# Prompt attention scores on 64 partitions at one place of each unit, and smaller first weight pieces, in a hybrid decoder layer on one Trainium2 core

## Chip, cores and metric

The kernel runs on one core of a Trainium2 chip. The metric is the device time in microseconds (us) of one execution. Everything is float32 at the interface. Inside, TensorE (PE) takes most operands as pairs of float32r numbers, a high part "hi" and the rest "lo", so that a product of two float32 matrices becomes three products: hi·hi, hi·lo and lo·hi.

## What is computed

One decoder layer for 1024 prompt tokens and 32 sample tokens (8 sequences of 4), with shared weights. Cut to what matters here:

```python
xn = rms_norm(h, norm_g)
z = xn @ w_in                       # 1024 -> 6656 columns
u, zp, q, k, v, za, ga, gb = jnp.split(z, IN_SPLIT_POINTS, axis=-1)
ya = multiscale_pool(u_pad, pos, pool_map, pool_scale) * jax.nn.silu(zp)
q = rope(rms_norm(q ...), pos)      # 16 heads of 64
k = rope(rms_norm(k ...), pos)      # 4 key heads, 4 query heads share each
# prompt: blocks of 128 queries against the previous and the own block of 128 keys
s = einsum(q, k) * 64 ** -0.5       # per head and block: 128 x 64 times 64 x 256
pr = exp(s - m) / (sum(exp(s - m)) + exp(sink - m))
o = einsum(pr, v)
yb = o * jax.nn.silu(za)
m = sigmoid(ga) * (ya @ w_proj_pool) + sigmoid(gb) * (yb @ w_proj_attn)
h = h + m @ w_out
h = h + sigmoid(h @ w_ple_gate) * (p_l @ w_ple)
```

## The kernel before

Each engine has its own program, written out by hand in order; semaphores tie them together. The order in which a function is written is the order in which its engine works. A `wait_ge` on PE stops every later PE instruction.

**The projections.** Weights come in chunks of 256 columns, each as two pieces `raw_a` and `raw_b` of 512 KB. SP (SyncE) issues the transfers (`load_chunk`), POOL (GpSimd) splits them into `w_hi` and `w_lo` (`split`), and PE multiplies (`project` calls `products`). A tile of 128 output columns takes eight steps k; a step is nine products of 352 columns: six with `w_hi`, three with `w_lo`. They accumulate in banks 0 to 2 or 3 to 5 of PSUM (`ps`), in turn. Banks 6 and 7 are left for everything else.

**The start.** SP loads the identity, x block 0, the first weight piece, x blocks 1 and 2, the second piece, and the other x blocks. PE transposes x in units (`turn_unit`) and multiplies each at once with the first chunk (`unit_products`). ACT (ScalarE) and DVE (VectorE) make the first four k of `w_hi` and `w_lo`; POOL makes the other four (k 4 to 7) when `raw_b` has come.

**The q, k, v stage.** 45 token blocks (`token_block`, number n) go to bank `n % 6`, and ACT empties each (`take_block`). Then the first gate tile starts in banks 0 to 2 once all of them have been taken (`block_free` at `8 * PAIRS`).

**Prompt attention.** There are 32 units: 8 token blocks times 4 key heads, four query heads g to a unit. A unit's PE work lies between the steps of a projection tile, two units to a tile (`attention_half`, `after[k]` is called when step k is through). For unit u these are:
- the scores S(u, s), s = 0, 1: bank for two heads each. In `qt` a query head lies with its hi part on partitions 0 to 63 and its lo part on 64 to 127; in `kt` both halves of the partitions hold the same 64 rows of the keys, once as hi (part 0) and once as lo (part 1). Two products of 128 partitions per head give all four combinations.
- the transposes T(u, s) of the probabilities (`turn_probs`), four each, one unit later;
- the values V(u) (`values`): four products of 512 columns; the third and fourth need `pt_lo` of T(u, 1).

All of them share banks 6 and 7 in rounds: `round_of` waits on `att_read`, which counts the rounds that have been read, so that each round waits for the one before the last. In order these are S(u,0), S(u,1), T(u-1,0), T(u-1,1), V(u-1). So S(u+1,1) waits for V(u-1) to be read. ACT and DVE do the rest: DVE masks the scores (`mask_scores`), ACT takes the exponentials (`exps`), copies the transposed probabilities to `pt_hi` (`hi_probs`), DVE makes `pt_lo` (`split_probs`); V is read by ACT (`low_half`, into `kv_flat`) and then by DVE, which adds (into `ps`) and multiplies twice (into `sa`) in `gate_output`.

Of the kernel before, what the change touches and what calls it, by code (L numbers as in the profile page):

```python
# [21 lines left out]
F32 = mybir.dt.float32  # L22
F32R = mybir.dt.float32r
ALU = mybir.AluOpType
# [3 lines left out]
P = 128  # L28
D = 1024
KT = D // P  # L30
# [101 lines left out]
def round_number(kind, j, i):  # L132

    return {"rows": 6 * j, "rms": 3, "back": 9 + 3 * j}[kind] + i

# [47 lines left out]
def build(nc, xp, xs, cache_k, cache_v, state, pp, ps_, params, w_in, pool_map, w_pp, w_pa, w_out, w_ple,  # L183
          w_gate, const, masks, smask, y_p, y_s, nk_p, nv_p, npool_p, nk_s, nv_s, npool_s):
    with ExitStack() as ctx:
# [119 lines left out]
        group_done, za_done, old_put, zp_done = sem("group_done"), sem("za_done"), sem("old_put"), sem("zp_done")  # L305
        paired, block_done, block_free, s_low_done, s_added = (
# [67 lines left out]
        def _(sp):  # L374
# [10 lines left out]
            def load_half(h):  # L385
                src = w_in[512 * h:512 * h + 512, COL["k"]:COL["k"] + WC].rearrange("(k p) n -> p k n", p=P)
                sp.dma_start(raw[h][:], src).then_inc(raw_loaded[h], 16)
# [6 lines left out]
            load_half(0)  # L394
            for t in range(1, 3):
                load_x(t)
            load_half(1)
# [5 lines left out]
            sp.dma_start(state_rows[0:NB * HIST, :], state).then_inc(hist_loaded, 16)  # L403
            load_chunk(1, w_in, COL["q"])
# [148 lines left out]
        def _(pool):  # L553
# [15 lines left out]
            def chunk(n, slot, end, m=None, used=tile_done):  # L569
                if not isinstance(n, int) or n != QKV_CHUNK:  # L570
                    split(n, slot, end, 0, 0, 4, n, used)
# [19 lines left out]
            for n in range(3):  # L591
                chunk(n, n % 2, chunk_end(0) if n == 2 else 0)
# [11 lines left out]
        def _(pe):  # L604
            def project(parity, free, slot, f, src_hi, src_lo, wait_m=None, used=False, k0=0, kn=KT,
                        pieces=None, after=None, done=False):
# [6 lines left out]
                for k in range(kn):  # L613
# [5 lines left out]
                    last = products(parity, slot, f, src_hi, src_lo, k, k0, kn)  # L619
# [9 lines left out]
            def products(parity, slot, f, src_hi, src_lo, k, k0=0, kn=KT):  # L629

                wh = w_hi[:, slot, k0 + k, P * f:P * f + P]
                wl = w_lo[:, slot, k0 + k, P * f:P * f + P]
                for w, parts in ((wh, (src_hi, src_lo)), (wl, (src_hi,))):
                    for c in range(NCH):
                        for x in parts:
                            last = nc.tensor.matmul(  # L636
                                ps[:, 3 * parity + c, 0:CH], w, x[:, k, CH * c:CH * c + CH],
                                start=(k == 0 and w is wh and x is src_hi), stop=(k == kn - 1 and w is wl))
                return last
# [14 lines left out]
            def unit_products(i):  # L654
# [8 lines left out]
                if g == 0 and k % 4 == 0:  # L663
                    pe.wait_ge(piece_split[k // 4], 1)
# [84 lines left out]
            def token_block(c, p):  # L749

                n, t, slot = 9 * (c - 1) + p, PAIR_BLOCKS[p], c % 2
                if n < 6:
                    pe.wait_ge(set_free[n // 3], 1)
# [8 lines left out]
                for k in range(KT):  # L762
# [10 lines left out]
                    for a, (m, x, w) in enumerate(parts):  # L773
                        last = nc.tensor.matmul(ps[0:m, n % 6, 0:WC], x, w, start=(k == 0 and a == 0),  # L774
# [70 lines left out]
            pe.wait_ge(block_free, 8 * PAIRS)  # L845
            pe.wait_ge(s_added, PAIRS)
            for i in range(2):
                for h in range(4):
# [8 lines left out]
                    else:  # L857
                        after = {4: [lambda v=v: turn_sample_probs(v)],
# [13 lines left out]
            def scores(u, m, t, s, first=False):  # L872
# [4 lines left out]
                if s == 0:  # L877
                    pe.wait_ge(unit_loaded[kv], t * 48 + 48)
                bank = round_of("S", u, s, m, first)
# [1102 lines left out]
```

## Time and profile before

| | us |
|---|---|
| median of 3 runs | 1184.72 (1183.96 to 1185.47) |
| the profiled execution's own time | 1184.52 |
| its span, first to last instruction | 1182.7 |
| PE busy | 1173.5 (99% of the span) |
| DVE, ACT, POOL busy | 571.2, 404.4, 406.0 |

The profile is of one execution. A busy time of PE holds overlaps: matmuls are pipelined, and the end of each is modelled, so what a matmul costs is read from the distance between the starts of neighbours and not from its own duration. The span is 1.8 us shorter than the execution's time. The stages, by the stretches of the trace: the start to 41.5 us, the q, k, v stage to 178, the first gates with the sample attention to 287.7, prompt attention to 566, and the pooling branch, the projections and the output to the end.

### The profile page before, as it was taken

The numbers are of one execution on the slowest core, as the hardware profiler recorded it, in microseconds if no ns is written. First come the engines' busy times: TensorE is split into PE (matmuls) and PEld (weight loads), VectorE is DVE, ScalarE is ACT, GpSimd is POOL, SyncE is SP. The second block draws the span as 40 slices with busy tenths as digits, with TensorE's granted clock in tenths as the row PEclk, the third lists the DMA queues.
The fourth block names the chain that finished last, engine by engine and source line by source line (L and its number), as shares of the span: only waits on it lengthen the run. The fifth ranks groups of instructions, "written<-read, shape, count | busy, mean of one in ns | idle before, by whom it ended". The sixth has DMA issues, their size and how long they took to land.

```text
span 1182.7 us, 19808 instructions
## 1 busy us (share of the span) xinstructions
PE 1173.5 (99%) x7720; PEld 1156.2 (98%) x7720; DVE 571.2 (48%) x1012; ACT 404.4 (34%) x922; POOL 406.0 (34%) x187
## 2 busy tenths in 40 slices
PE   8999999999999999999999999999999999999998
PEld 7999999999999999999999999999999999999998
DVE  6567773112556555565546283852264360163322
ACT  6433333233676776766110000221130130031112
POOL 3333333333212222221345333333533443274310
PEclk9999999999999999999999999999999999999999
DMA  9425466212444434423511211063222332322211
GB/s 298 166 72 159 143 164 198 63 54 74 120 122 119 136 101 132 116 81 101 201 50 56 65 47 38 2 240 126 75 88 84 115 122 79 112 87 63 64 37 55
DMA packets 115807, 124.92 MB, mean 106 GB/s; under 512 B 14192, under 2 KB 104456, under 8 KB 115744
## 3 DMA queue, kind: packets, MB, share of 16 engines
q1 hardware_dynamic: 100935, 100.22, 27.2%
q10 hardware_dynamic: 14808, 23.82, 7.3%
q8 instruction: 44, 0.72, 0.3%
q14 instruction: 20, 0.16, 0.0%
HBM read 88.93 MB, written 37.12 MB: 107 GB/s over the span
## 4 chain that ended last, share of the span: by engine, by line
PE 98%; DMA 1%; POOL 0%; DVE 0%; ACT 0%; SPq 0%; issue 0%; DVEq 0%; ACTq 0%; POOLq 0%
PE ps L636 73%; PE ps L774 10%; PE ps L892 3%; PE ps L882 2%; PE ps L908 2%; PE ps L660 2%; PE ps L1030 1%; PE ps L736 1%; DMA raw_b<-in_w_in 1%; PE ps L999 1%; PE ps L650 0%; PE ps L840 0%; PE ps L820 0%; POOL w_lo L566 0%; ACT prob L1754 0%; POOL w_hi L564 0%
## 5 line engine op out<-in xcount | busy, mean ns | idle before, releaser
L636 PE MATMUL ps<-m_hi,w_hi 128*128 128x352 f32 x1704 | 557.1, 328 | 0.5 <-ACT sa L1593 0.5
L636 PE MATMUL ps<-m_lo,w_hi 128*128 128x352 f32 x1704 | 548.0, 322 | 0.0
L636 PE MATMUL ps<-m_hi,w_lo 128*128 128x352 f32 x1704 | 367.5, 323 | 0.0
L636 PEld LDWEIGHTS ps<-m_hi,w_hi 128*128 128x128 f32 x1704 | 320.9, 188 | 3.1 <-ACT sa L1593 0.7
L636 PEld LDWEIGHTS ps<-m_lo,w_hi 128*128 128x128 f32 x1704 | 320.5, 188 | 1.4
L564 POOL TENSOR_TENSOR w_hi<-raw_a,w_one 128x1024 fp32r<-128x1024 f32 x41 | 79.0, 1927 | 703.8 <-PE ps L636 406.3
L636 PEld LDWEIGHTS ps<-m_hi,w_lo 128*128 128x128 f32 x1704 | 291.1, 188 | 0.0
L566 POOL TENSOR_TENSOR w_lo<-raw_b,w_hi 128x1024 fp32r<-128x1024 f32 x42 | 115.2, 2743 | 3.3
L566 POOL TENSOR_TENSOR w_lo<-raw_a,w_hi 128x1024 fp32r<-128x1024 f32 x41 | 103.3, 2519 | 3.2
L774 PE MATMUL ps<-w_lo,m_hi 128*128 128x256 f32 (+1 forms) x360 | 99.4, 282 | 0.0
L564 POOL TENSOR_TENSOR w_hi<-raw_b,w_one 128x1024 fp32r<-128x1024 f32 x42 | 90.8, 2161 | 10.8 <-DMA raw_b<-in_w_in 10.8
L774 PE MATMUL ps<-w_hi,m_hi 128*128 128x256 f32 x320 | 92.3, 288 | 0.0
L774 PE MATMUL ps<-w_hi,m_lo 128*128 128x256 f32 x320 | 89.9, 281 | 0.0
L1279 DVE TENSOR_TENSOR pt_lo<-ps,pt_hi 128x512 fp32r<-128x512 f32 x64 | 44.2, 691 | 48.2 <-ACT pt_hi L1740 48.2
L1851 ACT ACTIVATE gin<-gin 128x1056 f32<-128x1056 f32 x16 | 17.4, 1088 | 144.9 <-DVE gin L1405 144.9
L1740 ACT ACTIVATE pt_hi<-ps 128x512 fp32r<-128x512 f32 x64 | 38.2, 599 | 82.2 <-PE ps L892 82.2
L774 PEld LDWEIGHTS ps<-w_lo,m_hi 128*128 128x128 f32 (+1 forms) x360 | 64.5, 179 | 0.1
L1754 ACT ACTIVATE prob<-prob,st 128x257 f32<-128x257 f32 x128 | 63.4, 501 | 0.0
L1269 DVE CUSTOM_DVE_ANT_0 prob<-ps,msk,sinks_n 128x256 f32<-128x256 f32 x128 | 56.7, 481 | 9.5 <-issue 9.1
L774 PEld LDWEIGHTS ps<-w_hi,m_lo 128*128 128x128 f32 x320 | 60.5, 189 | 0.0
L774 PEld LDWEIGHTS ps<-w_hi,m_hi 128*128 128x128 f32 x320 | 60.2, 188 | 0.1
L1767 ACT ACTIVATE prob<-prob,st 128x256 f32<-128x256 f32 x128 | 54.3, 497 | 0.1
(238 smaller groups left out, 1392.6 us busy)
## 6 DMA issues: line engine op xcount, KB each, us to landing
raw_a<-in_w_in SPq DMA_DIRECT2D x26, 512.0 KB, 4.0
raw_b<-in_w_in SPq DMA_DIRECT2D x26, 512.0 KB, 4.3
qk_d<-qkst ACTq DMA_DIRECT2D x20, 512.0 KB, 5.6
gate_d<-gst ACTq DMA_DIRECT2D x16, 528.0 KB, 3.5
gin<-gate_d SPq DMA_DIRECT2D x16, 528.0 KB, 3.7
qt<-qk_d SPq DMA_DIRECT2D x32, 256.0 KB, 3.6
yb_d<-sa SPq DMA_DIRECT2D x1, 4224.0 KB, 13.8
sa<-yb_d SPq DMA_DIRECT2D x1, 4224.0 KB, 15.7
```

Source lines behind the costliest of these rows:

```text
L564: hi_count.did(nc.gpsimd.tensor_tensor(hi, raw[piece][:], one, ALU.mult))
L566: nc.gpsimd.tensor_tensor(lo, raw[piece][:], hi.bitcast(F32), ALU.subtract)\
L636: last = nc.tensor.matmul(ps[:, 3 * parity + c, 0:CH], w, x[:, k, CH * c:CH * c + CH], start=(k == 0 and w is wh and x is src_hi), stop=(k ...
L660: return nc.tensor.matmul(ps[:, 3 * h + g, 0:n], wt[:, 0, k, P * h:P * h + P], x[:, k, c0:c0 + n], start=start, stop=(k == KT - 1 and x is ...
L774: last = nc.tensor.matmul(ps[0:m, n % 6, 0:WC], x, w, start=(k == 0 and a == 0), stop=(k == KT - 1 and a == len(parts) - 1))
L882: last = nc.tensor.matmul(ps[:, bank, 256 * (g % 2):256 * (g % 2) + 256], qt[:, slot, g, :], kt[:, kv, part, :, :].rearrange("p s n -> p ( ...
L892: last = nc.tensor.transpose(ps[:, bank, P * g:P * g + P], prob[:, m % 2, g, P * s:P * s + P], ident)
L1269: last = v.tensor_tensor_reduce(prob[:, slot, g, 0:2 * P], ps[:, bank, 256 * (g % 2):256 * (g % 2) + 256], msk[:, mask, :], -1.0, sinks_n[ ...
L1279: v.tensor_tensor(pt_lo[s][:], ps[:, bank, :], pt_hi[s][:].bitcast(F32), ALU.subtract)\
L1740: a.activation(pt_hi[s][:], ps[:, bank, :], ACT.Copy).then_inc(pt_hi_done, 1)
L1754: last = a.activation(prob[:, slot, g, 0:2 * P + 1], prob[:, slot, g, 0:2 * P + 1], ACT.Exp, bias=st[:, slot, 0, g:g + 1], scale=-1.0, acc ...
L1767: last = a.activation(prob[:, slot, g, 0:2 * P], prob[:, slot, g, 0:2 * P], ACT.Copy, scale=st[:, slot, 5, g:g + 1])
```

## The change

1. **Scores.** `qt` now holds, on each half of the partitions, two of the four heads: partitions 0 to 63 heads 0 and 1, partitions 64 to 127 heads 2 and 3, each as hi and lo next to each other. A head takes three products of 64 partitions (hi·hi, lo·hi, hi·lo; lo·lo is dropped). The twelve products of a unit alternate between the halves, and with them between banks 6 and 7, and all stand at one place. The transfer of `qt` becomes four of 64 partitions.
2. **Places.** `fine` calls after each third product, not only after a step. Unit by unit: scores after step k0, T(u-1,0) nine products later, T(u-1,1) six products after that, V(u-1) six products after that; then 15 products to the next scores.
3. **ACT's order.** The exponentials of the first two heads come ahead of `hi_probs`, the other two behind it.
4. **First pieces.** The first chunk comes in four quarters of 256 KB. ACT and DVE split the first (k 0 and 1), POOL the other three.
5. **Bank of a token block.** `(n + 3) % 6` instead of `n % 6`. ACT frees banks 3 to 5 before 0 to 2 at the start; the last three blocks now lie in banks 3 to 5, and the first gate tile waits for 37 taken blocks instead of 40.

```diff
+def block_bank(n):
+    return (n + 3) % 6
...
+            def load_quarter(i):
+                src = w_in[256 * i:256 * i + 256, COL["k"]:COL["k"] + WC].rearrange("(k p) n -> p k n", p=P)
+                h, second = divmod(i, 2)
+                sp.dma_start(raw[h][:, 2 * second:2 * second + 2, :], src)\
+                    .then_inc(raw_loaded[h] if second else early_raw[h], 16)
...
             load_x(0)
-            load_half(0)
+            load_quarter(0)
             for t in range(1, 3):
                 load_x(t)
-            load_half(1)
+            for i in range(1, 4):
+                load_quarter(i)
...
-                sp.dma_start(qt[:, m % 2, :, :].bitcast(F32),
-                             qk_d[G * kv:G * kv + G, :, tok].rearrange("g p n -> p g n")).then_inc(unit_loaded[kv], 16)
+                for half in range(2):
+                    for s in range(2):
+                        sp.dma_start(qt[HD * half:HD * half + HD, m % 2, 2 * s:2 * s + 2, :].bitcast(F32),
+                                     qk_d[G * kv + 2 * half:G * kv + 2 * half + 2, HD * s:HD * s + HD, tok]
+                                     .rearrange("g e n -> e g n")).then_inc(unit_loaded[kv], 16)
...
+            def split_quarter(i):
+                h, second = divmod(i, 2)
+                pool.wait_ge(raw_loaded[h] if second else early_raw[h], 16)
+                src = raw[h][:, 2 * second:2 * second + 2, :]
+                hi, lo = w_hi[:, 0, 2 * i:2 * i + 2, :], w_lo[:, 0, 2 * i:2 * i + 2, :]
...
-            pe.wait_ge(block_free, 8 * PAIRS)
+            pe.wait_ge(block_free, blocks_taken(PAIRS, 5))
...
-                for g in (2 * s, 2 * s + 1):
-                    for part in range(2):
-                        last = nc.tensor.matmul(ps[:, bank, 256 * (g % 2):256 * (g % 2) + 256], qt[:, slot, g, :],
-                                                kt[:, kv, part, :, :].rearrange("p s n -> p (s n)"),
-                                                start=(part == 0), stop=(part == 1))
-                last.then_inc(att_done, 1)
+                banks = [round_of("S", u, s, m, first) for s in range(2)]
+                for g in range(2):
+                    for a, (q_part, k_part) in enumerate(((0, 0), (1, 0), (0, 1))):
+                        for s in range(2):
+                            half = slice(HD * s, HD * s + HD)
+                            last = nc.tensor.matmul(ps[:, banks[s], 256 * g:256 * g + 256],
+                                                    qt[half, slot, 2 * q_part + g, :],
+                                                    kt[half, kv, k_part, :, :].rearrange("p s n -> p (s n)"),
+                                                    start=(a == 0), stop=(a == 2))
+                            if g == 1 and a == 2:
+                                last.then_inc(att_done, 1)
...
-                after = {k0: [], k0 + 1: [], k0 + 2: [], k0 + 3: []}
-                after[k0].append(lambda: scores(u, m, t, 0, first and m == 0))
-                after[k0 + 1].append(lambda: scores(u, m, t, 1, first and m == 0))
+                fine = {3 * k0 + 2: [lambda: scores(u, m, t, first and m == 0)]}
                 if not first or m >= 1:
-                    after[k0 + 1].append(lambda: turn_probs(u - 1, (m - 1) % 8, 0))
-                    after[k0 + 2].append(lambda: turn_probs(u - 1, (m - 1) % 8, 1))
-                    after[k0 + 3].append(lambda: values(u - 1, (m - 1) % 8, t if m % 4 else t - 1))
+                    fine[3 * k0 + 5] = [lambda: turn_probs(u - 1, (m - 1) % 8, 0)]
+                    fine[3 * k0 + 7] = [lambda: turn_probs(u - 1, (m - 1) % 8, 1)]
+                    fine[3 * k0 + 9] = [lambda: values(u - 1, (m - 1) % 8, t if m % 4 else t - 1)]
...
                     u = i * 8 + m
+                    exps(u, m, 0)
                     if not first or m >= 1:
                         u_slot[0] = (m - 1) % 8
                         hi_probs(u - 1)
-                    exps(u, m)
+                    exps(u, m, 1)
```

PE, second unit of the attention stage, in the kernel before (L882 are the scores, L636 the projection's products, L892 the transposes, L908 the values; shapes are those of the result):

```order
L882 MATMUL ps<-kt,qt 128x256 [waits att_read,unit_loaded1]
L882 MATMUL ps<-kt,qt 128x256 x3
L636 MATMUL ps<-m_hi,w_hi 128x352
L636 MATMUL ps<-m_lo,w_hi 128x352
L636 MATMUL ps<-m_hi,w_hi 128x352
L636 MATMUL ps<-m_lo,w_hi 128x352
L636 MATMUL ps<-m_hi,w_hi 128x352
L636 MATMUL ps<-m_lo,w_hi 128x352
L636 MATMUL ps<-m_hi,w_lo 128x352 x3
L882 MATMUL ps<-kt,qt 128x256 [waits att_read]
L882 MATMUL ps<-kt,qt 128x256 x3
L892 MATMUL ps<-con_s,prob 128x128 [waits att_read,prob_done]
```

The same place with the change (L915 are the scores, L663 the products, L927 the transposes):

```order
L915 MATMUL ps<-kt,qt 128x256 [waits att_read,unit_loaded1]
L915 MATMUL ps<-kt,qt 128x256 x11
L663 MATMUL ps<-m_hi,w_hi 128x352
L663 MATMUL ps<-m_lo,w_hi 128x352
L663 MATMUL ps<-m_hi,w_hi 128x352
L663 MATMUL ps<-m_lo,w_hi 128x352
L663 MATMUL ps<-m_hi,w_hi 128x352
L663 MATMUL ps<-m_lo,w_hi 128x352
L663 MATMUL ps<-m_hi,w_lo 128x352 x3
L927 MATMUL ps<-con_s,prob 128x128 [waits att_read,prob_done]
```

Eight products at two places have become twelve at one, and both waits of the scores now stand ahead of the first of them.

PE, from the second set of transposes to the values in the same unit, before:

```order
L892 MATMUL ps<-con_s,prob 128x128 [waits att_read]
L892 MATMUL ps<-con_s,prob 128x128 x3
L636 MATMUL ps<-m_hi,w_hi 128x352
L636 MATMUL ps<-m_lo,w_hi 128x352
L636 MATMUL ps<-m_hi,w_hi 128x352
L636 MATMUL ps<-m_lo,w_hi 128x352
L636 MATMUL ps<-m_hi,w_hi 128x352
L636 MATMUL ps<-m_lo,w_hi 128x352
L636 MATMUL ps<-m_hi,w_lo 128x352 x3
L908 MATMUL ps<-pt_hi,vt 128x512 [waits zero_done,v_loaded0,att_read]
L908 MATMUL ps<-pt_lo,vt 128x512
L908 MATMUL ps<-pt_hi,vt 128x512 [waits att_read]
```

And with the change (L943 are the values):

```order
L927 MATMUL ps<-con_s,prob 128x128 [waits att_read]
L927 MATMUL ps<-con_s,prob 128x128 x3
L663 MATMUL ps<-m_hi,w_lo 128x352 x3
L663 MATMUL ps<-m_hi,w_hi 128x352
L663 MATMUL ps<-m_lo,w_hi 128x352
L663 MATMUL ps<-m_hi,w_hi 128x352
L943 MATMUL ps<-pt_hi,vt 128x512 [waits zero_done,v_loaded0,att_read]
L943 MATMUL ps<-pt_lo,vt 128x512
L943 MATMUL ps<-pt_hi,vt 128x512 [waits att_read]
```

Between these transposes and the first product of the values stand six projection products instead of nine.

SP's first transfers, before:

```order
L392 DMA con_s<-in_const 128x128
L390 DMA xr<-in_x_prompt 128x1024
L387 DMA raw_a<-in_w_in 128x4x256
L390 DMA xr<-in_x_prompt 128x1024 x2
L387 DMA raw_b<-in_w_in 128x4x256
L390 DMA xr<-in_x_prompt 128x1024 x5
```

And with the change:

```order
L400 DMA con_s<-in_const 128x128
L398 DMA xr<-in_x_prompt 128x1024
L394 DMA raw_a<-in_w_in 128x2x256
L398 DMA xr<-in_x_prompt 128x1024 x2
L394 DMA raw_a<-in_w_in 128x2x256
L394 DMA raw_b<-in_w_in 128x2x256 x2
L398 DMA xr<-in_x_prompt 128x1024 x5
```

256 KB instead of 512 KB of weights now stand ahead of x blocks 1 and 2.

## Rows read from the trace of the kernel before

**Rows 1.** The page: span, busy time of each engine, and the chain by engine.

```profile
span 1182.7 us, 19808 instructions
...
PE 1173.5 (99%) x7720; PEld 1156.2 (98%) x7720; DVE 571.2 (48%) x1012; ACT 404.4 (34%) x922; POOL 406.0 (34%) x187
...
PE 98%; DMA 1%; POOL 0%; DVE 0%; ACT 0%; SPq 0%; issue 0%; DVEq 0%; ACTq 0%; POOLq 0%
```

**Rows 2.** The attention stretch: us, busy time of PE, PEld, DVE, ACT, POOL, clock, DMA.

```profile
287.70:566.00 278.30, 278.07 (x1808) 269.21 (x1807) 156.55 (x510) 193.77 (x530) 71.58 (x34) 1.00 0.40 111
```

**Rows 3.** Timeline, one unit: start, length, engine, line, operation, count, idle before.

```profile
408.58 0.63 PE L882 MATMUL ps<-kt,qt 128*128 128x256 f32 x4
409.11 0.66 PE L892 MATMUL ps<-con_s,prob 128*128 128x128 f32 x4
...
411.05 0.60 PE L892 MATMUL ps<-con_s,prob 128*128 128x128 f32 x4
...
411.65 0.32 PE L636 MATMUL ps<-m_lo,w_hi 128*128 128x352 f32 x1
...
412.32 0.69 DVE L1279 TENSOR_TENSOR pt_lo<-ps,pt_hi 128x512 fp32r<-128x512 f32 x1 [1.20 <-ACT pt_hi L1740]
...
412.95 0.40 PE L908 MATMUL ps<-pt_hi,vt 128*128 128x512 f32 x1
...
413.41 0.39 PE L908 MATMUL ps<-pt_hi,vt 128*128 128x512 f32 x1
...
413.64 0.40 PE L908 MATMUL ps<-pt_lo,vt 128*128 128x512 f32 x1
...
413.88 0.32 PE L636 MATMUL ps<-m_hi,w_hi 128*128 128x352 f32 x1
...
414.27 0.60 ACT L1761 ACTIVATE kv_flat<-ps 64x512 f32<-64x512 f32 x1
...
415.31 0.64 PE L882 MATMUL ps<-kt,qt 128*128 128x256 f32 x4
...
415.79 0.32 PE L636 MATMUL ps<-m_hi,w_hi 128*128 128x352 f32 x1
...
415.81 0.85 DVE L1293 TENSOR_TENSOR sa<-ps,sa 64x256 f32 x2
```

**Rows 4.** Timeline around products on 64 partitions (L822) and on 32 (L837).

```profile
190.45 0.28 PE L820 MATMUL ps<-kts,q_pair 128*128 128x128 f32 x1
190.66 0.29 PEld L822 LDWEIGHTS ps<-q_sum 64*128 64x128 f32 x2
...
190.99 0.19 PEld L636 LDWEIGHTS ps<-m_hi,w_hi 128*128 128x128 f32 x1
...
191.26 0.32 PE L636 MATMUL ps<-m_lo,w_hi 128*128 128x352 f32 x1
...
204.19 0.32 PE L636 MATMUL ps<-m_hi,w_lo 128*128 128x352 f32 x1
204.44 0.29 PEld L837 LDWEIGHTS ps<-spt,v_group 32*128 32x128 f32 x2 [0.22 <-issue]
...
204.66 0.27 PE L837 MATMUL ps<-spt,v_group 32*128 32x128 f32 x1
204.86 0.19 PEld L840 LDWEIGHTS ps<-spt,vc 128*128 128x128 f32 x1
```

**Rows 5.** Timeline of the start: idle times of PE, and POOL's split.

```profile
8.75 0.88 PE L650 MATMUL ps<-con_s,xr 128*128 128x128 f32 x6 [1.47 <-DMA xr<-in_x_prompt]
10.08 0.88 PE L650 MATMUL ps<-con_s,xr 128*128 128x128 f32 x6 [0.23 <-DMA xr<-in_x_prompt]
...
16.07 0.19 PEld L660 LDWEIGHTS ps<-m_hi,w_hi 128*128 128x128 f32 x1 [0.28 <-POOL w_lo L566]
```

**Rows 6.** Timeline where the first gate tile begins.

```profile
177.97 0.43 PE L636 MATMUL ps<-m_hi,w_hi 128*128 128x352 f32 x1 [0.46 <-ACT sa L1593]
```

**Rows 7.** Timeline of SP: what issuing two transfers of 64 partitions takes.

```profile
401.29 1.31 SPq L454 DMA_DIRECT2D kt<-qk_d  x2
```

More of the change, by code:

```diff
@@ L305, in build @@
         group_done, za_done, old_put, zp_done = sem("group_done"), sem("za_done"), sem("old_put"), sem("zp_done")
+        early_raw, early_split = ([sem(f"early_{x}{i}") for i in range(2)] for x in ("raw", "split"))
         paired, block_done, block_free, s_low_done, s_added = (
@@ L569, in chunk @@
             def chunk(n, slot, end, m=None, used=tile_done):
-                if not isinstance(n, int) or n != QKV_CHUNK:
-                    split(n, slot, end, 0, 0, 4, n, used)
+                split(n, slot, end, 0, 0, 4, n, used)
                 split(n, slot, end, 1, 4, 4, n, used)
@@ L589, in chunks @@
                 hi_count.leave(count // 2 - 1, steps)
-            for n in range(3):
-                chunk(n, n % 2, chunk_end(0) if n == 2 else 0)
+            def split_quarter(i):
[3 more added lines that the diff above has]
+                hi, lo = w_hi[:, 0, 2 * i:2 * i + 2, :], w_lo[:, 0, 2 * i:2 * i + 2, :]
+                hi_count.did(nc.gpsimd.tensor_tensor(hi, src, w_one[:, 0:1].unsqueeze(2).to_broadcast([P, 2, WC]),
+                                                     ALU.mult))
+                hi_count.settle()
+                nc.gpsimd.tensor_tensor(lo, src, hi.bitcast(F32), ALU.subtract)\
+                    .then_inc(piece_split[h] if second else early_split[h], 1)
+            for i in range(1, 4):
+                split_quarter(i)
+            chunk(1, 1, 0)
+            chunk(2, 0, chunk_end(0))
             for n in range(3, GATE_CHUNK):
@@ L618, in project @@
                         pe.wait_ge(m_ready, wait_m + (k + 1))
-                    last = products(parity, slot, f, src_hi, src_lo, k, k0, kn)
+                    last = products(parity, slot, f, src_hi, src_lo, k, k0, kn, fine)
                     if used and k < kn - 1:
@@ L638, in products @@
                                 start=(k == 0 and w is wh and x is src_hi), stop=(k == kn - 1 and w is wl))
+                            count += 1
+                            if fine and count % 3 == 0:
+                                for call in fine.get(3 * k + count // 3 - 1, ()):
+                                    call()
                 return last
@@ L773, in token_block @@
                     for a, (m, x, w) in enumerate(parts):
-                        last = nc.tensor.matmul(ps[0:m, n % 6, 0:WC], x, w, start=(k == 0 and a == 0),
+                        last = nc.tensor.matmul(ps[0:m, block_bank(n), 0:WC], x, w, start=(k == 0 and a == 0),
                                                 stop=(k == KT - 1 and a == len(parts) - 1))
@@ L870, in round_of, with scores @@
                 return 6 + (att_bank(kind, m, first) + s) % 2
-            def scores(u, m, t, s, first=False):
+            def scores(u, m, t, first=False):
                 slot, kv = m % 2, m % 4
@@ L1154, in add_sample_rows @@
                 dve.wait_ge(s_low_done, c)
[L1155 removed]
+                bank = block_bank(9 * (c - 1) + 4)
                 parts = ps[0:NS, bank, 0:WC].rearrange("p (s n) -> p s n", s=2)
```

55 lines of the change are left out of this document (27 added, 28 removed).

## The prediction

> **What bounds the kernel now.** I read the page first. The reader should see in [rows 1] that PE is busy 99% of the span and makes up 98% of the chain that ended last, while no other engine reaches half. So whatever shortens PE's own work, or one of its few idle times, shortens the kernel, and whatever makes PE wait lengthens it one for one. The stretch of attention [rows 2] then shows the same for the stage that the change edits most: 278.07 us busy of 278.30, at full clock. PE waits for nobody there now. The timeline of a unit [rows 3] gives prices as distances between starts. A unit's eight score products cost 0.48 us at one place (415.31 to 415.79) and 0.53 at the other (408.58 to 409.11), so 1.01 in all; one of them is 0.12 (0.48/4). A projection product is 0.162 ((412.95 - 411.65)/8). The start [rows 5] and the first gate tile [rows 6] hold the idle times that the change could remove.
>
> **The start.** PE waits 1.47 and 0.23 us for x blocks 1 and 2. Between their arrivals 512 KB more have come in 1.33 us (8.75 to 10.08), so 256 KB less in front of them bring both forward by 0.67. The other wait, 0.28 for POOL's split of k 4 to 7, goes if POOL keeps up with quarters: it can begin with the quarter right behind x block 2, while now it waits for the whole second piece, and the work for two k is half of that for four. Gain together 0.9; bounds 0 (the transfers come in another order) and 1.2.
>
> **Banks and the first gate tile.** PE's 0.46 us wait for ACT [rows 6] is for the last taken block. With the last three blocks in banks 3 to 5 and 37 instead of 40 required, it goes: 0.5. At the other end ACT now frees banks 3 to 5 first, behind eight history transposes of PE that cover the copy; without that cover it would cost one copy, a few tenths. I take 0.
>
> **Transfers of `qt`.** Four of 64 partitions instead of one of 128. Two such take SP 1.31 us to issue [rows 7], so three more are about 2 us per unit. SP issues a unit's loads two units ahead (about 17 us, a unit being 278/32 = 8.7), and it has only seven transfers a unit to issue. The weights' loads queue behind them by 2 us, and POOL splits one chunk in two tiles. No cost.
>
> **The scores themselves.** Two terms.
> First the switch. [Rows 4] hold the only products of fewer than 128 partitions. Going in: L820 starts at 190.45, the next weight load could start then, but the load for the 64-partition product starts at 190.66, 0.21 later; for L837 the previous product starts at 204.19, its stream ends at 204.35, and the load begins at 204.44, so that the first product starts about 0.20 late. Coming out: two of these loads take 0.29 where one takes 0.19, so the second starts at 190.76 and its product at 190.86, yet the next load waits until 190.99 (0.13); behind L837's second product (204.66) the load that would normally start with it starts at 204.86 (0.20). In and out cost 0.34 and 0.40; I take 0.37 per unit, where the 128-partition scores pay nothing (starts run through at 0.12 and 0.16).
> Second the twelve products. Nothing in this trace has two products on different halves next to each other, so the bounds are: six pairs side by side, 6 x 0.12 = 0.72; or all twelve one after the other, 12 x 0.12 = 1.44. In between, weight loads in a row: two of them on 64 partitions stand 0.10 apart [rows 4], so twelve are 1.20. Nearest rows are of products that all used one half; they say nothing against two halves at once, and the alternation uses two banks and two sets of rows. I take the pairs, at odds of about three to two.
> A unit then costs 0.72 + 0.37 = 1.09 against 1.01: +0.08, times 32 = +2.6 us. One after the other it is 1.20 + 0.37 = 1.57 (+0.56, +18 us) to 1.44 + 0.37 = 1.81 (+0.80, +26 us).
> The Trainium skill ("TensorEngine Tiling (Array Packing)", Key Properties) says that different tiles can run weight loads and matmuls in parallel, and that changing the tiling mode drains the engine. By the first half of the rule the sum is that of the pairs; by [rows 4] alone, with loads in a row, it would be 15 us more. This trace agrees with the second half (0.34 and 0.40) and shows nothing of the first.
>
> **The waits that move.** The chain behind T(u-1,1) has a fixed length. From the start of its transposes (411.05) to the end of DVE's `pt_lo` (412.32 + 0.69 = 413.01) it is 1.96 us, with ACT and DVE free. PE now reaches the third product of V at 413.41, 2.36 after, so there is 0.4 of slack. With six products in between instead of nine, PE is there at (411.65 - 0.16 - 411.05) + 6 x 0.162 + 0.46 = 1.87, and its weight load should start 0.11 before that, at 1.76. The load waits behind the semaphore: a stall of 0.2, 31 times, +6 us. ACT and DVE don't gain or lose here: the exponentials of the first two heads end ahead of this copy, the others come after it.
> The chain behind V: from the start of its last product (413.64) to the end of DVE's multiplication (415.81 + 0.85 = 416.66) it is 3.02, in which ACT started 0.23 after the product's end (413.64 + 0.40 to 414.27). With two exponentials behind `hi_probs` instead of four ACT is free, so about 2.82. S(u+1,1) waits for this; now it stands a whole step behind S(u+1,0), so that it has slack. With both banks wanted at once, PE is there after 0.24 + 15 x 0.162 = 2.67, and after the 0.09 that emptying the array takes (204.35 to 204.44) the load could start at 2.76. A stall of 0.1, 31 times, +3 us. Queued behind either stall is all of PE's work; no other engine waits for it in a way that the chain would show. Lower bound of both 0, if ACT and DVE are a little quicker than in this unit; upper bound twice as much.
>
> **The sum.** Against the profiled execution, 1184.5 (span 1182.7 and 1.8 around it; the median of the runs is 1184.7): 1184.5 - 0.9 - 0.5 + 2.6 + 6 + 3 = 1194.7. I say 1195.
>
> **The rivals.**
> - *No overlap of the halves* (or the weight loads in a row): 1194.7 + 15 to + 23 = 1210 to 1218. For it: loads 0.10 apart on one half are all that the trace has. Against it: 64 partitions leave half of the array free, and the twelve products alternate so that neighbours share neither rows nor bank.
> - *Pairs and no stalls*: 1184.5 - 1.4 + 2.6 = 1185.7, no change. For it: the two stalls are differences of 0.1 and 0.2 us between chains of 2 to 3. Against it: 1.96 for the `pt_lo` chain is made of operations that waited for nothing else.
> - *Faster: the switch costs nothing next to pairs.* If a pair's first load can start while the 128-partition products drain, the scores cost 0.72 for 1.01, so -0.29 x 32 = -9.3; with the gains of the start and without stalls 1174, with both stalls 1183. It decides from the point where the switch in and out costs under 0.3 us and the stalls stay under half of what I gave them. Against it stand the four transitions of [rows 4], each 0.13 to 0.21.
> - *The change does not bring twelve products down to pairs because nothing sets the array up for halves.* Then the twelve run one by one without a switch: 12 x 0.12 - 1.01 = 0.43, +13.8, with the start's gains and both stalls 1206. L822's 0.21 speaks against it.
>
> **How the numbers follow.** Pairs with stalls (1189 to 1200) 0.45; no overlap, with or without stalls (1201 to 1218) 0.30; pairs without stalls (1182 to 1188) 0.12; the fast case 0.08; the rest, such as no switch and no overlap, 0.05. The predicted time is that of the first. The range goes from 1184 to 1217: it takes in the no-overlap case but for its edge, and most of the case without stalls. The likeliest case has 1189 to 1200 of its own. A measurement of this kernel tells 0.2% (2.4 us) from no change, so: faster 0.10, same 0.10, slower 0.80.
>
> **What would show it.** Scores: in the timeline the twelve L915 products either start in pairs a few ns apart, the group of twelve about 0.6 us long from first to last start, or 0.10 to 0.12 apart, 1.1 to 1.3 us long. The switch: the load behind them starts 0.1 after the last stream. Stalls: PE idle in front of L943 with DVE `pt_lo` as releaser, and in front of L915 with DVE `sa`, which [rows 1] had nowhere. Start: x block 2's transposes at about 9.4 instead of 10.08, and no wait for POOL's `w_lo`. First gate tile: no idle time. It would be wrong if the switch were free, if the halves did not overlap, or if the two stalls did not appear.

## The result and the profile after

The changed kernel takes 1197.07 us (median of 4 runs, 1196.62 to 1197.63) against 1184.39 for the kernel before (1183.96 to 1185.47). The ratio is 1.0105, 95% interval 1.0092 to 1.0117. So it is 12.7 us slower. The forecast was 1195 in a range of 1184 to 1217.

The page of the changed kernel (span 1195.0 us): busy times, and the chain by engine.

```profile
PE 1185.8 (99%) x7848; PEld 1148.3 (96%) x7848; DVE 565.5 (47%) x1012; ACT 405.6 (34%) x922; POOL 408.8 (34%) x191
...
PE 94%; DVE 3%; ACT 1%; issue 1%; DVEq 0%; DMA 0%; ACTq 0%
```

PE is "busy" 99% in both kernels [rows 1] and yet this one waits. What gives it away is the chain, where PE fell from 98% to 94% while DVE rose from 0% to 3% and ACT from 0% to 1%, and PEld, the weight loads, which fell from 98% of the span to 96%. The ends of matmuls are modelled, and one that started before a wait covers it. A wait of 0.2 us is seen on the loads, not on the products. The waits of PEld, with total, times and longest:

```profile
PEld ps L943 <- DVE pt_lo L1312: 12.7, 31, 0.4
PEld ps L915 <- DVE sa L1326: 8.3, 24, 0.4
...
PEld ps L915 <- issue: 2.6, 8, 0.7
```

31 times in front of the third product of the values, and 24 + 8 in front of the scores. An idle time of 0.41 here is not 0.41 lost, since a load is also idle while the product ahead streams. What is lost is read from distances. One unit of the changed kernel, cut where it says `...` (L943 values, L915 scores, L927 transposes, L663 projection products):

```profile
408.56 0.39 PE L943 MATMUL ps<-pt_lo,vt 128*128 128x512 f32 x1
...
410.52 0.85 DVE L1326 TENSOR_TENSOR sa<-ps,sa 64x256 f32 x2
...
410.72 0.65 PE L663 MATMUL ps<-m_hi,w_lo 128*128 128x352 f32 x3
...
411.42 0.78 PEld L915 LDWEIGHTS ps<-kt,qt 64*128 64x128 f32 x12 [0.35 <-DVE sa L1326]
411.42 0.98 PE L915 MATMUL ps<-kt,qt 64*128 64x256 f32 x12
412.33 0.19 PEld L663 LDWEIGHTS ps<-m_hi,w_hi 128*128 128x128 f32 x1
...
412.60 0.32 PE L663 MATMUL ps<-m_lo,w_hi 128*128 128x352 f32 x1
...
415.28 0.60 PE L927 MATMUL ps<-con_s,prob 128*128 128x128 f32 x4
...
416.55 0.69 DVE L1312 TENSOR_TENSOR pt_lo<-ps,pt_hi 128x512 fp32r<-128x512 f32 x1 [0.70 <-ACT pt_hi L1773]
...
416.93 0.40 PE L943 MATMUL ps<-pt_lo,vt 128*128 128x512 f32 x1
417.29 0.19 PEld L943 LDWEIGHTS ps<-pt_hi,vt 128*128 128x128 f32 x1 [0.41 <-DVE pt_lo L1312]
...
417.63 0.39 PE L943 MATMUL ps<-pt_lo,vt 128*128 128x512 f32 x1
```

- From the transposes' start to the end of `pt_lo`: 415.28 to 416.55 + 0.69 = 417.24, 1.96 us, exactly as before [rows 3]. The load that waits for it starts at 417.29. The second and the fourth product of the values now start 0.70 apart (416.93 to 417.63), where it was 0.46 before (2 x 0.23 [rows 3]): 0.24 lost in each unit.
- From the last product of the values to the end of DVE's multiplication: 408.56 to 411.37, 2.81. The scores' load starts at 411.42. The last projection product ahead of it starts at 411.05 (410.72 + 0.65 - 0.32) and streams until 411.21.
- From that 411.21 to the next projection product's stream (412.60 - 0.16 = 412.44) the scores cost 1.23, against 1.01 at two places before: 0.22 more, of which about 0.12 is waiting (where nothing holds it, the load starts 0.09 after the stream's end, as in e3 below; that would be 411.30, and it starts at 411.42).

The unit is 9.07 us long (408.56 to 417.63), for 8.7 before. Now the start, and where the first gate tile begins (L805 is the last product of the q, k, v stage, L769 the last transpose of q's last pair, L841 the first transposes of the keys, later in the same gate tile):

```profile
9.07 0.82 PE L681 MATMUL ps<-con_s,xr 128*128 128x128 f32 x6
...
10.18 0.41 PE L691 MATMUL ps<-m_hi,w_hi 128*128 128x384 f32 x1 [0.28 <-ACT m_hi L1579]
...
175.76 0.28 PE L805 MATMUL ps<-w_hi,m_lo 128*128 128x256 f32 x1
...
175.91 0.41 PE L663 MATMUL ps<-m_hi,w_hi 128*128 128x352 f32 x1
...
179.70 1.29 DVE L1182 TENSOR_TENSOR qkst<-ps,qkst 128x512 fp32r<-128x512 f32 x2 [2.03 <-ACT qkst L1642]
...
180.45 0.33 PE L769 MATMUL ps<-con_s,sa 128*128 128x128 f32 x1 [0.52 <-DVE qkst L1182]
...
184.97 0.60 PE L841 MATMUL ps<-con_s,kc 128*128 128x128 f32 x4
```

The same place in the kernel before (L774, L738 and L810 are those three products):

```profile
177.13 0.28 PE L774 MATMUL ps<-w_hi,m_lo 128*128 128x256 f32 x1
...
181.07 1.29 DVE L1149 TENSOR_TENSOR qkst<-ps,qkst 128x512 fp32r<-128x512 f32 x2 [2.03 <-ACT qkst L1609]
...
181.84 0.31 PE L738 MATMUL ps<-con_s,sa 128*128 128x128 f32 x1
...
186.34 0.60 PE L810 MATMUL ps<-con_s,kc 128*128 128x128 f32 x4
```

x block 2's transposes start at 9.07 instead of 10.08 [rows 5]. The first gate tile starts without a wait: 0.15 behind the last product of the stage (175.76 to 175.91), for 0.84 before (177.13 to 177.97 [rows 6]), so 0.69 is gained. But 4.5 us later PE waits 0.52 for DVE before the last transpose of q's last pair (L769), a wait that the trace of before doesn't list. DVE's operation for it starts 3.94 behind the last product of the stage in both kernels (175.76 to 179.70, 177.13 to 181.07). Only PE comes sooner, and the gain is given back in full: from the last product of the stage to the keys' transposes it is 9.21 in both (175.76 to 184.97, 177.13 to 186.34).

### The profile page after: what moved, and what is told of

Its sections match the earlier page's. It is cut to its first block, busy times and chain, and to the rows that moved or that the text cites. A ratio compares the mean times of both kernels' runs of the same rounds, so it can differ in the third digit from the quotient of the medians.

```text
span 1195.0 us, 20288 instructions
## 1 busy us (share of the span) xinstructions
PE 1185.8 (99%) x7848; PEld 1148.3 (96%) x7848; DVE 565.5 (47%) x1012; ACT 405.6 (34%) x922; POOL 408.8 (34%) x191
## 4 chain that ended last, share of the span: by engine, by line
PE 94%; DVE 3%; ACT 1%; issue 1%; DVEq 0%; DMA 0%; ACTq 0%
PE ps L663 68%; PE ps L805 10%; PE ps L943 3%; PE ps L915 3%; PE ps L927 2%; PE ps L691 2%; DVE ps L1321 1%; PE ps L1063 1%; ACT kv_flat L1796 1%; DVE sa L1326 1%; PE ps L681 1%; PE ps L767 1%; PE ps L1032 1%; PE ps L871 0%; PE ps L714 0%
## 5 line engine op out<-in xcount | busy, mean ns | idle before, releaser
L663 PE MATMUL ps<-m_hi,w_hi 128*128 128x352 f32 x1704 | 558.1, 328 | 0.0
L663 PE MATMUL ps<-m_lo,w_hi 128*128 128x352 f32 x1704 | 548.2, 322 | 0.0
L663 PE MATMUL ps<-m_hi,w_lo 128*128 128x352 f32 x1704 | 370.2, 325 | 0.0
L663 PEld LDWEIGHTS ps<-m_hi,w_hi 128*128 128x128 f32 x1704 | 320.9, 188 | 6.4
L663 PEld LDWEIGHTS ps<-m_lo,w_hi 128*128 128x128 f32 x1704 | 320.5, 188 | 1.4
L663 PEld LDWEIGHTS ps<-m_hi,w_lo 128*128 128x128 f32 x1704 | 290.1, 188 | 0.0
L805 PE MATMUL ps<-w_lo,m_hi 128*128 128x256 f32 (+1 forms) x360 | 99.4, 282 | 0.0
L805 PE MATMUL ps<-w_hi,m_hi 128*128 128x256 f32 x320 | 92.2, 288 | 0.0
L805 PE MATMUL ps<-w_hi,m_lo 128*128 128x256 f32 x320 | 89.9, 281 | 0.0
L805 PEld LDWEIGHTS ps<-w_lo,m_hi 128*128 128x128 f32 (+1 forms) x360 | 64.5, 179 | 0.1
L805 PEld LDWEIGHTS ps<-w_hi,m_lo 128*128 128x128 f32 x320 | 60.5, 189 | 0.0
L805 PEld LDWEIGHTS ps<-w_hi,m_hi 128*128 128x128 f32 x320 | 60.2, 188 | 0.1
```

Of the source, the lines that this page charges most:

```text
L663: last = nc.tensor.matmul(ps[:, 3 * parity + c, 0:CH], w, x[:, k, CH * c:CH * c + CH], start=(k == 0 and w is wh and x is src_hi), stop=(k ...
L805: last = nc.tensor.matmul(ps[0:m, block_bank(n), 0:WC], x, w, start=(k == 0 and a == 0), stop=(k == KT - 1 and a == len(parts) - 1))
```

## The experiments

Each is an edit of the changed kernel, or of an experiment that is named. The diffs are cut to what matters. Times are medians; the kernel before took 1184.2, 1184.4 and 1184.1 us in the three groups of runs.

**e1. The attention of before.** Only quarters and banks are left of the change; the products of the scores and the one transfer of `qt` are also those of before.

```diff
-                fine = {3 * k0 + 2: [lambda: scores(u, m, t, first and m == 0)]}
+                after[k0].append(lambda: scores(u, m, t, 0, first and m == 0))
+                after[k0 + 1].append(lambda: scores(u, m, t, 1, first and m == 0))
...
-                    exps(u, m, 0)
                     if not first or m >= 1:
                         u_slot[0] = (m - 1) % 8
                         hi_probs(u - 1)
-                    exps(u, m, 1)
+                    exps(u, m)
```

> The changed kernel with the attention of before (scores on 128 partitions at two places, one transfer for qt, the exponentials behind hi_probs); the quarters and the bank shift stay. My theory, from the changed kernel's trace: the start is worth about 1.1 us (first product at 10.18 instead of 11.23), and the bank shift 0, because the 0.5 us that PE no longer waits for ACT at the first gate tile comes back as 0.52 us before L769, which waits for DVE. So about 1183.3. As I predicted before the result: 1.4 us for both, 1183.0. The rival that makes the first pieces worthless, since the gain is lost further on: 1184.4.

1183.6 us, ratio 0.9990 (0.9981 to 0.9999); the span is 1181.6 for 1182.7. PE waits 0.5 us before that late transpose here too. So the start and the banks together are worth 0.6 us by the medians, 1.1 by the spans and 1.2 by the ratio: the kernel before has some runs at 1185.5 to 1186.4 which the median leaves out. The attention costs the changed kernel 13.5 us (1197.07 - 1183.6).

**e2. Second transposes three products earlier.**

```diff
-                    fine[3 * k0 + 7] = [lambda: turn_probs(u - 1, (m - 1) % 8, 1)]
+                    fine[3 * k0 + 6] = [lambda: turn_probs(u - 1, (m - 1) % 8, 1)]
```

> The changed kernel, with the second set of transposes three products earlier (nine products between it and the values instead of six, three instead of six behind the first set). Theory of the stall: PE's 0.24 us wait in front of the third product of the values goes in each of 31 units, 7.4 us, so about 1189.7. Rival, the 64-partition products themselves carry the loss: 1197, no change. Rival, T1 now waits for the masks of the second score bank: also 1197 or worse.

1189.73 us, ratio 1.0044 (1.0028 to 1.0059): 7.3 us less than the changed kernel. The wait before L943 is gone from the list, that before the scores is the same (first row), and the load of the third product starts with the second product, at 414.38:

```profile
PEld ps L915 <- DVE sa L1326: 8.4, 24, 0.4
```

```profile
414.38 0.19 PEld L943 LDWEIGHTS ps<-pt_hi,vt 128*128 128x128 f32 x1
```

One number in the source carries more than half of the loss.

**e3. Everything else of a unit earlier.**

```diff
-                    fine[3 * k0 + 5] = [lambda: turn_probs(u - 1, (m - 1) % 8, 0)]
-                    fine[3 * k0 + 7] = [lambda: turn_probs(u - 1, (m - 1) % 8, 1)]
-                    fine[3 * k0 + 9] = [lambda: values(u - 1, (m - 1) % 8, t if m % 4 else t - 1)]
+                    fine[3 * k0 + 4] = [lambda: turn_probs(u - 1, (m - 1) % 8, 0)]
+                    fine[3 * k0 + 5] = [lambda: turn_probs(u - 1, (m - 1) % 8, 1)]
+                    fine[3 * k0 + 8] = [lambda: values(u - 1, (m - 1) % 8, t if m % 4 else t - 1)]
```

> The changed kernel with the first transposes six products behind the scores, the second three behind them, the values nine behind these, and so 18 products to the next scores. Theory of the stalls: both waits go (0.24 in front of the values, 0.12 in front of the scores), 31 x 0.36 = 11 us, so 1186. If the first set then waits for ACT or DVE, only part of it: 1190. Rival, the 64-partition scores carry the loss: 1197.

1190.57 us, ratio 1.0052 (1.0036 to 1.0067), the middle one of the three cases. Both old waits are gone, but the first transposes wait:

```profile
409.65 0.32 PE L663 MATMUL ps<-m_lo,w_hi 128*128 128x352 f32 x1
...
409.90 0.42 PEld L927 LDWEIGHTS ps<-con_s,prob 128*128 128x128 f32 x4 [0.22 <-DVE st L1302]
...
416.10 0.64 PE L663 MATMUL ps<-m_hi,w_lo 128*128 128x352 f32 x3
...
416.67 0.77 PEld L915 LDWEIGHTS ps<-kt,qt 64*128 64x128 f32 x12 [0.22 <-issue]
...
417.85 0.32 PE L663 MATMUL ps<-m_lo,w_hi 128*128 128x352 f32 x1
```

The projection's stream ends at 409.65 + 0.16 = 409.81, the transposes' at best begins at 409.90 + 0.11 = 410.01: 0.20 lost in this unit. The scores, now without a wait, cost 417.85 - 0.16 - (416.10 + 0.64 - 0.32 + 0.16) = 1.11.

**e4. The eight products on 128 partitions, at the one place.** The old layout and the one transfer of `qt` come with them.

```diff
-                    for a, (q_part, k_part) in enumerate(((0, 0), (1, 0), (0, 1))):
-                        for s in range(2):
-                            half = slice(HD * s, HD * s + HD)
-                            last = nc.tensor.matmul(ps[:, banks[s], 256 * g:256 * g + 256],
-                                                    qt[half, slot, 2 * q_part + g, :],
-                                                    kt[half, kv, k_part, :, :].rearrange("p s n -> p (s n)"),
-                                                    start=(a == 0), stop=(a == 2))
+                for s in range(2):
+                    for g in range(2):
+                        for part in range(2):
+                            last = nc.tensor.matmul(ps[:, banks[s], 256 * g:256 * g + 256], qt[:, slot, 2 * s + g, :],
+                                                    kt[:, kv, part, :, :].rearrange("p s n -> p (s n)"),
+                                                    start=(part == 0), stop=(part == 1))
...
```

> The changed kernel with the scores of before, eight products of 128 partitions and the old layout of qt, but still at one place and with the changed places of everything else. My theory: the group costs 8 x 0.12 = 0.96 instead of 1.11, so 0.15 a unit less, minus a scores' stall that grows by 0.09 since PE arrives without having to empty: 32 x 0.06 = 2 us less, 1195. Rival, the switch and the 64-partition products carry the loss: 11 us less, 1186.

1197.96 us, ratio 1.0112 (1.0097 to 1.0128). Not 2 us less but 0.9 more. The waits are the changed kernel's, to 0.1 us:

```profile
PEld ps L937 <- DVE pt_lo L1306: 12.8, 31, 0.4
PEld ps L911 <- DVE sa L1320: 8.3, 24, 0.4
```

```profile
409.09 0.39 PE L937 MATMUL ps<-pt_lo,vt 128*128 128x512 f32 x1
...
411.96 1.01 PEld L911 LDWEIGHTS ps<-kt,qt 128*128 128x128 f32 x8 [0.35 <-DVE sa L1320]
...
413.01 0.32 PE L660 MATMUL ps<-m_hi,w_hi 128*128 128x352 f32 x1
```

The chain behind the values sets the instant of the scores' first load in both kernels: 2.87 after the last product of the values here (409.09 to 411.96), 2.86 in the changed kernel (408.56 to 411.42). Whatever going in costs there lies inside that wait. From the load to the next projection product it is 1.05 here (411.96 to 413.01) and 1.02 there (411.42 to 412.44): what the pairs gain, coming out takes back. The halves and the switch cost nothing *with the places of the changed kernel*; there the places make the whole loss.

**e5. Six products of the lower half, then six of the upper.** The same twelve.

```diff
-                for g in range(2):
-                    for a, (q_part, k_part) in enumerate(((0, 0), (1, 0), (0, 1))):
-                        for s in range(2):
...
+                for s in range(2):
...
+                    for g in range(2):
+                        for a, (q_part, k_part) in enumerate(((0, 0), (1, 0), (0, 1))):
...
```

> The changed kernel with the same twelve products of 64 partitions, but first the six of the lower half, then the six of the upper half, so that no neighbours but one pair use different halves. Theory of the pairs: the group grows from 0.72 to 1.44 less one product, +0.6 a unit, +19 to +22 us: 1216 to 1219. Rival, the halves overlap whatever the order is, since the queue looks ahead: 1197. The stall of the values stays; that of the scores too.

1208.09 us, ratio 1.0201 (1.0185 to 1.0216): 11 us more, between the two expectations.

```profile
415.67 1.11 PEld L915 LDWEIGHTS ps<-kt,qt 64*128 64x128 f32 x12 [0.35 <-DVE sa L1325]
...
416.92 0.19 PEld L663 LDWEIGHTS ps<-m_hi,w_hi 128*128 128x128 f32 x1
```

From the first load to the one behind the group it is 1.25, where it was 0.91 with the halves in turn (411.42 to 412.33): 0.34 x 32 = 10.9. Twelve loads within 1.11, less one load's 0.18, are 0.085 apart, closer than the 0.12 of one product behind the other on one half. So part of the upper half's products ran beside the lower half's, though they stand behind them in the program.

**e6. ACT's old order.**

```diff
-                    exps(u, m, 0)
                     if not first or m >= 1:
                         u_slot[0] = (m - 1) % 8
                         hi_probs(u - 1)
+                    exps(u, m, 0)
                     exps(u, m, 1)
```

> The changed kernel, with all four exponentials behind hi_probs on ACT, as before. Theory: hi_probs of the first set starts earlier, which nobody needs; the copy for V (low_half) waits for two more exponentials, about 0.5 to 1 us longer behind the transposes, so it starts some 0.2 us later than PE's values allow, and the stall in front of the scores grows from 0.12 to about 0.3: +5 us, 1202. Rival, ACT's order is without effect: 1197.

1210.54 us, ratio 1.0222 (1.0207 to 1.0238): 13.5 us more, where 5 were expected.

```profile
413.89 0.39 PE L943 MATMUL ps<-pt_lo,vt 128*128 128x512 f32 x1
...
414.16 0.50 ACT L1788 ACTIVATE prob<-prob,st 128x257 f32<-128x257 f32 x1
...
414.77 0.59 ACT L1796 ACTIVATE kv_flat<-ps 64x512 f32<-64x512 f32 x1
...
417.21 0.78 PEld L915 LDWEIGHTS ps<-kt,qt 64*128 64x128 f32 x12 [0.80 <-DVE sa L1326]
```

ACT is at its exponentials until 414.7 and takes up the values' result 0.88 us after the last product's start (413.89 to 414.77) instead of the 0.42 that are possible (408.56 to 408.98 in the changed kernel). The wait before the scores grows from 0.35 to 0.80, and 0.45 x 31 = 14. With ACT's old order the change of places would have cost as much again.

**e7. e3's places with e4's products.**

> Scores of before on 128 partitions, all eight at one place, and everything else three to six products earlier as in e3. Theory: without stalls, against the kernel before only the start's gain is left, and the group of eight costs the same as its two halves: 1183.3. Against e3 it shows what the halves cost with the switch: 0.15 x 32 = 5 us. Rival, scores at one place hold PE up by themselves: above 1187.

1180.64 us, ratio 0.9968 (0.9957 to 0.998): faster than the kernel before by 3.7 us, 9.9 under e3 and 3.0 under e1, which keeps the places of before. That is 2.7 less than expected.

```profile
413.44 1.11 PE L911 MATMUL ps<-kt,qt 128*128 128x256 f32 x8
...
414.39 0.32 PE L660 MATMUL ps<-m_hi,w_hi 128*128 128x352 f32 x1
...
415.19 0.32 PE L660 MATMUL ps<-m_lo,w_hi 128*128 128x352 f32 x1
...
415.36 0.60 PE L921 MATMUL ps<-con_s,prob 128*128 128x128 f32 x4
```

Everything runs through: the scores cost 0.95 (413.44 to 414.39), the transposes follow the projection product by 0.17. Against e3 that is 1.11 - 0.95 = 0.16 from the halves with their switch, 5.1 us in 32 units. The wait of the first transposes in e3 is 0.15 on average over the units (0.20 in the one shown), 4.7 us in 31. Together that is 9.8 for the measured 9.9.

The 3.0 us under e1 are a wait that the kernel before has in its attention, and e1 too. The list of waits doesn't show it:

```profile
408.56 0.48 DVE L1269 CUSTOM_DVE_ANT_0 prob<-ps,msk,sinks_n 128x256 f32<-128x256 f32 x1
...
409.10 0.42 PEld L892 LDWEIGHTS ps<-con_s,prob 128*128 128x128 f32 x4
```

T(u-1,0) stands directly behind S(u,1) and needs the bank of S(u,0), which DVE reads twice (`mask_scores`). The second reading ends at 408.56 + 0.48 = 409.04, and the load of the transposes starts 0.06 later. In 24 of the 31 units of the trace, from the eighth on, it follows by 0.06 or 0.07 as here. From the last projection product to the next, S(u,1) and T(u-1,0) together take 1.02 on average, where S(u,0) alone takes 0.47 and T(u-1,1) alone 0.44: 0.11 lost, 31 times 3.4 us. With the transposes six products behind the scores this is gone. So the sentence of the prediction that PE waits for nobody in this stage was not right: a busy PE had covered the wait.

**e8. e1 with the late transpose one step later.**

```diff
-                            after[1] = [lambda: turn("back", 9, 2)]
+                            after[2] = [lambda: turn("back", 9, 2)]
```

> As e1 (attention of before, quarters and bank shift), and the last of the three transposes of q's last pair one step (nine products) later in the first gate tile. Theory: the bank shift's 0.5 us was given back at this wait, so it now stays: 0.5 us under e1, 1182.8. Rival: it is given back once more further on, same as e1.

1182.82 us, ratio 0.9987 (0.9978 to 0.9996), 0.8 under e1; the wait is gone and the spans differ by 1.0 (1181.6 and 1180.6). The intervals of e1 and e8 overlap; the trace is clearer:

```profile
175.86 0.28 PE L802 MATMUL ps<-w_hi,m_lo 128*128 128x256 f32 x1
...
184.32 0.60 PE L838 MATMUL ps<-con_s,kc 128*128 128x128 f32 x4
```

From the last product of the q, k, v stage to the keys' transposes it is 8.46, where it was 9.21 in the kernel before and in the changed kernel: the 0.75 is kept.

**e9. e7 with e8's edit.**

> e7 (scores of before at one place, everything else of a unit earlier, quarters and bank shift) with the later transpose of e8. Theory: both gains add, 0.8 us under e7's 1180.6, so 1179.8 to 1180.2. Rival: PE's wait in front of that transpose is made up for later, 1180.6.

1180.39 us, ratio 0.9964 (0.9952 to 0.9976). The fastest of all, though not to be told from e7, and 0.2 us above what was expected.

**e10. e7 with the banks in turn.** Eight products on 128 partitions, in the order bank 6, bank 7, bank 6 and so on.

```diff
-                for s in range(2):
-                    for g in range(2):
-                        for part in range(2):
+                for g in range(2):
+                    for part in range(2):
+                        for s in range(2):
...
```

> e7, but the eight products of 128 partitions alternate between the two banks, so that the first bank is complete at the seventh product instead of the fourth. Theory of the late bank: DVE's first mask starts 0.35 us later, and the first transposes, which now find their bank read just in time, wait about 0.25 us in each of 31 units: +7 to +8 us over e7, 1188. Rival: e3's 10 us over e7 are all from the products on halves and the switch, and the order of the banks has no effect: 1180.6.

1187.98 us, ratio 1.0029 (1.0019 to 1.004): 7.3 us over e7, from nothing but the order of the same eight products.

```profile
418.66 0.32 PE L660 MATMUL ps<-m_lo,w_hi 128*128 128x352 f32 x1
...
418.99 0.42 PEld L922 LDWEIGHTS ps<-con_s,prob 128*128 128x128 f32 x4 [0.30 <-DVE st L1297]
```

The transposes' stream begins at 419.10 and could at 418.82: 0.28 lost in this unit, which 31 times would be 8.7. DVE's reading of the first bank is again what the transposes wait for.

**e11. e3's twelve products in two groups.**

```diff
-                fine = {3 * k0 + 2: [lambda: scores(u, m, t, first and m == 0)]}
+                fine = {3 * k0 + 1: [lambda: scores(u, m, t, 0, first and m == 0)],
+                        3 * k0 + 2: [lambda: scores(u, m, t, 1, first and m == 0)]}
```

> e3 with the twelve products on halves in two groups of six, three projection products between them (the first group stands three products earlier). Theory of the switch: one more switch in and out per unit, 0.37 to 0.40 us, plus about 0.1 of wait in front of the first group, since it stands nearer to the values: 32 x 0.37 + 31 x 0.1 = 15 us over e3, 1203 to 1206. Rival, the switch is only seen behind very short products and costs nothing next to pairs of 256 columns: 1191 to 1194.

1206.7 us, ratio 1.0186 (1.0171 to 1.0202), 16.1 over e3.

```profile
415.15 0.32 PE L663 MATMUL ps<-m_lo,w_hi 128*128 128x352 f32 x1
...
415.54 0.42 PEld L919 LDWEIGHTS ps<-kt,qt 64*128 64x128 f32 x6 [0.36 <-DVE sa L1331]
...
416.09 0.75 PE L663 MATMUL ps<-m_hi,w_lo 128*128 128x352 f32 x3
...
417.32 0.19 PEld L663 LDWEIGHTS ps<-m_hi,w_hi 128*128 128x128 f32 x1
```

The first group costs 416.09 + 0.11 - (415.15 + 0.16) = 0.89 and the second 417.32 + 0.11 - (416.09 + 0.75 - 0.33 + 0.16) = 0.76, together 1.65 where one group of twelve costs 1.11. 0.14 of the 0.54 is the wait for the values (0.36 idle for the 0.22 of a load that waits for nothing, as in e3), 0.40 is one more switch in and out.

## Why the prediction was right

It was 1195 (1194.7 worked out) for 1197.07 measured, with the likeliest case as the mechanism: the pairs form, and both waits appear where they were expected. Step by step:

- **Pairs.** Right. Twelve products take 0.98 from first start to last end, which less a product's modelled 0.28 and the first load's 0.11 is five steps of 0.12. Two in a pair start within 0.02 of each other. e5 shows what the order brings: 11 us of the 23 (32 x 0.72) that pairs save against twelve products one after the other; in e5 a part of the pairs still forms. The rule of the Trainium skill ("TensorEngine Tiling (Array Packing)", Key Properties) on tiles that load and multiply in parallel agrees with the loads here: twelve within 0.78 us, 0.055 apart.
- **The switch.** 0.37 was taken from four transitions of very short products; 0.40 was measured for one more (e11), and 0.16 for halves with switch against whole rows (e3 with e7), where 1.09 - 0.96 = 0.13 stood in the prediction's terms. Against the 1.01 of the two places, the term was +0.08, and the group without a wait measured 1.11, so +0.10.
- **The wait before the values.** 0.2 predicted, 0.24 measured by the distances; 6 us predicted, 7.3 by e2. The chain of 1.96 us was the same to 0.01.
- **The wait before the scores.** 0.1 predicted, about 0.12 measured; the chain of 2.82 came out as 2.81. What e4 adds: the emptying of the array lies inside this wait. In the prediction both stood in the sum, correctly, since the load can start only when both are over, but taking the halves away gains nothing then. So with the places as changed the waits are the cause of the slowdown, and the prediction had 9 of its 11.6 us of attention there. It is not the only way to put it: once the places are mended, the halves cost 9.9 us (e3 against e7), half of it by the halves with their switch and half by the wait of the first transposes, a wait that e10 brings about on whole rows by filling the two banks in turn.
- **The wait that was not seen.** The prediction priced the scores at 1.01 of the kernel before and took the stage to be without waits. Its timeline [rows 3] has 0.53 for the second four products, not 0.48, and then 0.66 for the transposes, not 0.60: both hold part of DVE's hold-up that e7 brings out. The change of places ends it, so by the averages of the two traces a unit gains 0.05 at the transposes and loses 0.23 at the values and 0.23 at the scores: 0.41, and 32 times 13.1 for the 13.5 measured. Against the prediction's terms that is 1.8 us more at the scores and 1.6 less at the transposes, which cancel; this much of the agreement is luck.
- **The start.** 0.9 predicted, of 0.67 for the x blocks and 0.28 for POOL. POOL's wait is gone from the changed kernel's trace; x block 2 came 1.01 earlier and the first product 1.05. Right in kind, but the size is not well known. All traces with the new start have the same code there, and the first token block starts at 39.51 (e3) to 40.70 (e10), so 0.8 to 2.0 earlier than the 41.53 of the one trace of before: the x blocks don't land at the same time in every execution (the transposes of x block 2 start at 8.29 in e3 and at 9.50 in e10).
- **The banks: wrong.** The step that fails is "with the last three blocks in banks 3 to 5 and 37 instead of 40 required, it goes: 0.5". The wait goes and 0.69 is gained, but 0.69 comes back before L769: it is worth 0. The prediction looked at the wait that ends and not at what stood behind it with no slack, which is ACT's and DVE's part for q's last pair, due at the same instant in both kernels. e8 takes it away.
- The total is 2.4 us too low: attention 13.5 for 11.6 (the values' wait 1.3 of it), and the start and banks 0.6 to 1.2 for 1.4.

What stays open: how much the first pieces save on average. In these runs it is somewhere about 1 us, and one trace of the kernel before is too little to say more.

## What to carry to other kernels

When PE is the bound, work inserted between its products has to be placed by the chains of the other engines, and the slack of every such chain is to be written down before anything is moved: here the best places (e7) and the worst with the same order of ACT (e4) differ by 17 us, while products on half the partitions cost nothing (e4) to 10 us (e3 against e7, half of it again a wait). A stage in which PE is busy 100% can still hold such waits: 0.1 us in each unit of the kernel before was in no list, and showed only when the distance of the same products was compared at two places (e7). Where two banks are filled at one place, fill them one after the other, since the reader of the first can start half a group earlier (e10, 7.3 us). Read waits of PE from its weight loads and from distances between starts.

## What was not expected of the hardware

In e5 the first product of the upper half, seventh in the program, starts at 416.0 beside the lower half's third, and the lower half's last, sixth in the program, is only the ninth to start (416.36). The group took 0.34 us more than with the halves in turn, where one after the other but for one neighbour pair would have been 5 x 0.12 = 0.6 more.
- Going to 64 partitions and back cost 0.40 us around 256-column products (e11), as around the very short ones in the kernel before (0.34 and 0.40 [rows 4]).
